# Twelve blocks of Strassen weight sums: from VectorE's program to one of GpSimd's own

## What is computed

```python
ODD_SPLITS = (RET_QK_W, RET_QK_W, RET_V_W, RET_V_W, MEM_W, MEM_W)   # 1024, 1024, 2048, 2048, 256, 256
h = rms_norm(x, norm_g)
rq, rk, rv, rz, eq, ez = _split(h @ w_in, ODD_SPLITS)
```

## Time and profile before

| | |
|---|---|
| median of three runs | 2156.94 us (2155.61 to 2162.51) |
| the profiled execution | 2156.11 us, span of its instructions 2154.3 us |
| TensorE busy | 2118.6 us, 98% of the span |
| weight loads of TensorE (beside its products) | 1171.6 us, 54% |
| VectorE busy | 755.4 us, 35% |
| ScalarE busy | 539.3 us, 25% |
| GpSimd busy | 0.2 us, four instructions |
| mean granted TensorE clock | 0.999 |

### The profile page before, as it was taken

One profiled execution on the slowest core, in us unless ns is written; L12 is line 12 of the kernel. 1 busy time (PEld: TensorE's weight loads), 2 busy tenths in 40 slices (PEclk: granted clock), 3 DMA queues, 4 the chain that ended last, 5 costly groups with the idle time before them and its releaser, 6 DMA issues.

```text
span 2154.3 us, 21143 instructions
## 1 busy us (share of the span) xinstructions
PE 2118.6 (98%) x8648; PEld 1171.6 (54%) x8648; DVE 755.4 (35%) x1215; ACT 539.3 (25%) x1065; POOL 0.2 (0%) x4
## 2 busy tenths in 40 slices
PE   8999999999999999999999999999999999999898
PEld 5555565647888777444544555554454443343247
DVE  3555544326665435312332434432140010100035
ACT  4755442320002223111223424330130100000024
POOL 0000000000000000000000000000000000000000
PEclk9999999999999999999999999999999999999999
DMA  8311211132222210233211111212639999999961
GB/s 209 76 40 40 78 40 52 45 119 79 78 80 87 74 54 22 75 80 70 96 61 61 57 40 40 72 57 78 234 137 381 409 409 409 409 409 409 409 266 40
DMA packets 162208, 316.64 MB, mean 147 GB/s; under 512 B 41216, under 2 KB 73088, under 8 KB 162112
## 3 DMA queue, kind: packets, MB, share of 16 engines
q1 hardware_dynamic: 159760, 313.29, 40.3%
q10 hardware_dynamic: 2352, 2.00, 0.4%
HBM read 312.83 MB, written 2.10 MB: 146 GB/s over the span
## 4 chain that ended last, share of the span: by engine, by line
PE 92%; DMA 4%; DVE 2%; ACT 1%; issue 1%; SPq 0%; DVEq 0%
PE bank L459 47%; PE bank L445 12%; PE bank L2701 9%; PE bank L2751 4%; PE bank L2615 2%; PE bank L2637 2%; PE bank L1262 2%; PE bank L1312 2%; PE bank L1284 2%; PE bank L1664 2%; DMA wide<-in_w_exp_up 1%; DMA ring<-in_w_exp_gate 1%; PE bank L2287 1%; PE bank L2277 1%; PE bank L2331 1%; DMA wide<-in_w_exp_down 1%
## 5 line engine op out<-in xcount | busy, mean ns | idle before, releaser
L459 PE MATMUL bank<-hT,ring 128*128 128x512 f32 (+1 forms) x1120 | 503.7, 599 | 5.8 <-DMA ring<-in_l_w_in 5.8
L459 PEld LDWEIGHTS bank<-hT,ring 128*128 128x128 f32 (+1 forms) x1120 | 205.3, 190 | 239.6 <-issue 237.1
L2701 PE MATMUL bank<-wide,xg 128*64 128x512 f32 x488 | 125.2, 595 | 4.0 <-DMA ring<-in_w_exp_gate 1.6
L445 PE MATMUL bank<-hT,ring 128*128 128x256 f32 x512 | 114.9, 379 | 0.0
L459 PE MATMUL bank<-rz,ring 128*128 128x512 f32 x256 | 111.4, 593 | 0.9 <-issue 0.9
L459 PE MATMUL bank<-ring,hT 128*128 128x512 f32 (+2 forms) x320 | 108.4, 494 | 0.0
L445 PEld LDWEIGHTS bank<-hT,ring 128*128 128x128 f32 x512 | 97.1, 190 | 17.2 <-issue 3.8
L2701 PE MATMUL bank<-ring,xg 128*64 128x512 f32 x352 | 100.5, 595 | 2.6 <-DMA ring<-in_w_exp_gate 1.5
L445 PE MATMUL bank<-l_quarter,l_quarter 128*128 128x256 f32 x384 | 87.2, 380 | 0.0
L2751 PE MATMUL bank<-wide,hidT 128*64 128x512 f32 x304 | 78.8, 596 | 3.7 <-DMA wide<-in_w_exp_down 2.9
L459 PEld LDWEIGHTS bank<-rz,ring 128*128 128x128 f32 x256 | 48.6, 190 | 62.0 <-issue 61.5
(11 more groups left out here) (474 smaller groups left out, 2766.8 us busy)
## 6 DMA issues: line engine op xcount, KB each, us to landing
wide<-in_w_exp_down SPq DMA_DIRECT2D x76, 512.0 KB, 13.5
ring<-in_l_w_in SPq DMA_DIRECT2D x18, 2048.0 KB, 7.8
wide<-in_w_exp_gate SPq DMA_DIRECT2D x68, 512.0 KB, 12.3
wide<-in_w_exp_up SPq DMA_DIRECT2D x54, 512.0 KB, 14.2
ring<-in_w_exp_up SPq DMA_DIRECT2D x50, 512.0 KB, 10.8
ring<-in_w_exp_down SPq DMA_DIRECT2D x42, 512.0 KB, 14.7
ring<-in_w_in SPq DMA_DIRECT2D x10, 2048.0 KB, 7.9
ring<-in_w_exp_gate SPq DMA_DIRECT2D x38, 512.0 KB, 13.3
```

The source lines that it names most:

```text
L445: mm = pe.matmul(self.out(n)[:, half * 256:half * 256 + 256], *halves[half][k], start=i == 0 and not job["goes_on"], stop=False, skip_grou ...
L459: mm = pe.matmul(self.out(n), *mats[i], start=i == 0, stop=i == len(mats) - 1)
L2701: mm = pe.matmul(bank[2 * which + n][e * 64:(e + 1) * 64, :], xg[p // 2 % 2][:, k, s:s + CAP], block_ap(j)[k % 2][:, n * 512:(n + 1) * 512 ...
```

## The change

The weight sums are taken out of VectorE's hooks and written as a program of GpSimd: `run_stages` gets a `gpsimd` function. It goes through the twelve blocks in order, and does for each `weight_sums` and `last_weight_sum`. GpSimd waits for the block's weights (`load_sem`), for the eviction of p4 of the block before (`free`, after which nothing reads s1 any more), and before the last sum for the eviction of p2 (`done_at[... + 2]`), which was the last reader of a12. s1 now counts on `weights_summed` too, and s2 waits for it there. The semaphore's numbers that TensorE waits for go up accordingly. Nothing else moves; the operations, their shapes and tiles are the same.

```diff
-        def run_stages(*stages):
+        def run_stages(*stages, gpsimd):
...
+                @block.gpsimd
+                def _(pool):
+                    gpsimd(pool)
...
-            def weight_sums(self, dve, j):
+            def weight_sums(self, pool, j, free):
                 a11, a12, a21, a22 = self.weights(j)
-                dve.wait_ge(*load_sem[j])
-                dveq(dve.tensor_tensor(self.s1, a21, a22, ALU.add))
-                dveq.wait(dve)
-                dve.tensor_tensor(self.s2, self.s1, a11, ALU.subtract).then_inc(weights_summed, 1)
-                dve.tensor_tensor(a21, a11, a21, ALU.subtract).then_inc(weights_summed, 1)
-
-            def last_weight_sum(self, dve, j, s2_at):
+                pool.wait_ge(*load_sem[j])
+                pool.wait_ge(*free)
+                pool.tensor_tensor(self.s1, a21, a22, ALU.add).then_inc(weights_summed, 1)
+                pool.wait_ge(weights_summed, self.before[j] + 1)
+                pool.tensor_tensor(self.s2, self.s1, a11, ALU.subtract).then_inc(weights_summed, 1)
+                pool.tensor_tensor(a21, a11, a21, ALU.subtract).then_inc(weights_summed, 1)
+
+            def last_weight_sum(self, pool, j, a12_used):
                 a12 = self.weights(j)[1]
-                dve.wait_ge(weights_summed, s2_at)
-                dve.tensor_tensor(a12, a12, self.s2, ALU.subtract).then_inc(weights_summed, 1)
-
...
+                pool.wait_ge(weights_summed, self.before[j] + 2)
+                pool.wait_ge(*a12_used)
+                pool.tensor_tensor(a12, a12, self.s2, ALU.subtract).then_inc(weights_summed, 1)
...
-                add(a21, self.b12, "dve", plus(c21, c12), [(weights_summed, w0 + 2), (quarters_made, self.first_made + 1)],
-                    hook=lambda dve, done: self.last_weight_sum(dve, j, w0 + 1))
-                add(self.s1, self.t1, "dve", plus(c22, c21),
-                    hook=None if following is None else lambda dve, done: self.weight_sums(dve, following))
+                add(a21, self.b12, "dve", plus(c21, c12), [(weights_summed, w0 + 3), (quarters_made, self.first_made + 1)])
+                add(self.s1, self.t1, "dve", plus(c22, c21))
...
-        run_stages(opening, Weave, out0, Second, lead2, Band, Linear, branches, Experts, tail, Store)
+        def weight_sums(pool):
+            free = out0.dense.done_at[cols1 - 1]
+            for dense, blocks in ((out0.dense, (1, 2, 3, 4, 5, 6, 12)), (dense1, range(7, 12))):
+                for b in blocks:
+                    j = ODD[b]
+                    q1.weight_sums(pool, j, free)
+                    q1.last_weight_sum(pool, j, dense.done_at[q1.at[j] + 2])
+                    free = dense.done_at[q1.at[j] + 4]
+
+        run_stages(opening, Weave, out0, Second, lead2, Band, Linear, branches, Experts, tail, Store, gpsimd=weight_sums)
```

More of the change, by code:

```diff
@@ L624, in __init__ @@
                 self.k, self.first_made = k, counts["quarters"] + 1
+                self.before, self.at = {}, {}
                 counts["quarters"] += 2
@@ L643, in weights, with block @@
                 return w[:, 0:k, 0:256], w[:, k:2 * k, 0:256], w[:, 0:k, 256:512], w[:, k:2 * k, 256:512]
-            def weight_sums(self, dve, j):
+            def weight_sums(self, pool, j, free):
                 a11, a12, a21, a22 = self.weights(j)
-                dve.wait_ge(*load_sem[j])
-                dveq(dve.tensor_tensor(self.s1, a21, a22, ALU.add))
-                dveq.wait(dve)
-                dve.tensor_tensor(self.s2, self.s1, a11, ALU.subtract).then_inc(weights_summed, 1)
-                dve.tensor_tensor(a21, a11, a21, ALU.subtract).then_inc(weights_summed, 1)
-            def last_weight_sum(self, dve, j, s2_at):
+                pool.wait_ge(*load_sem[j])
[5 more added lines that the diff above has]
+            def last_weight_sum(self, pool, j, a12_used):
                 a12 = self.weights(j)[1]
-                dve.wait_ge(weights_summed, s2_at)
-                dve.tensor_tensor(a12, a12, self.s2, ALU.subtract).then_inc(weights_summed, 1)
-            def block(self, jobs, j, c11, c12, c21, c22, banks=None, following=None, tokens_first=False, first=None,
+                pool.wait_ge(weights_summed, self.before[j] + 2)
+                pool.wait_ge(*a12_used)
+                pool.tensor_tensor(a12, a12, self.s2, ALU.subtract).then_inc(weights_summed, 1)
+            def block(self, jobs, j, c11, c12, c21, c22, banks=None, tokens_first=False, first=None,
                       lower=None, upper=None):
                 a11, a12, a21, a22 = self.weights(j)
-                w0 = counts["weights"]
-                counts["weights"] += 3
-                n0 = len(jobs)
+                w0 = self.before[j] = counts["weights"]
+                counts["weights"] += 4
+                n0 = self.at[j] = len(jobs)
                 def add(a, b, eng, evac, needs=(), goes_on=False, after=(), hook=None):
@@ L689, in block @@
                 add(a11, self.b11, "act", copied)
-                add(self.s2, self.t2, "dve", plus(c12, c11), [(weights_summed, w0 + 1), (quarters_made, self.first_made)], after=[0])
+                add(self.s2, self.t2, "dve", plus(c12, c11), [(weights_summed, w0 + 2), (quarters_made, self.first_made)], after=[0])
                 add(a12, self.b21, *(first or ("act", copied)), goes_on=True, after=[1])
-                add(a21, self.b12, "dve", plus(c21, c12), [(weights_summed, w0 + 2), (quarters_made, self.first_made + 1)],
-                    hook=lambda dve, done: self.last_weight_sum(dve, j, w0 + 1))
-                add(self.s1, self.t1, "dve", plus(c22, c21),
-                    hook=None if following is None else lambda dve, done: self.weight_sums(dve, following))
+                add(a21, self.b12, "dve", plus(c21, c12), [(weights_summed, w0 + 3), (quarters_made, self.first_made + 1)])
+                add(self.s1, self.t1, "dve", plus(c22, c21))
                 add(a22, self.t4, "dve", plus(c21, c21), hook=upper)
-                add(a12, self.b22, "dve", plus(c12, c12), [(weights_summed, w0 + 3)], goes_on=True, after=[2], hook=lower)
+                add(a12, self.b22, "dve", plus(c12, c12), [(weights_summed, w0 + 4)], goes_on=True, after=[2], hook=lower)
                 return n0
@@ L1504, in build @@
             first = fm1(ODD[i // 4], (i % 4) * P, to(rqk[i]), "act")
-            if i == 2:
-                jobs[first]["dve_then"] = lambda dve, done: q1.weight_sums(dve, ODD[1])
             if i == 0:
@@ L1541, in build @@
             q1.block(jobs, ODD[b], first[:, :, 0:256], first[:, :, 256:512], second[:, :, 0:256], second[:, :, 256:512],
-                     banks=banks_of[b % 3], following=ODD[b + 1], upper=turned_pair(second), lower=turned_pair(first))
+                     banks=banks_of[b % 3], upper=turned_pair(second), lower=turned_pair(first))
         def centre(c, ts, copied=None):
@@ L1564, in values_by_quarters @@
             q1.block(jobs, ODD[4 + c], v[:, 0:2, 0:256], v[:, 2:4, 0:256], v[:, 0:2, 256:512], v[:, 2:4, 256:512],
-                     banks=banks, following=following, tokens_first=True,
+                     banks=banks, tokens_first=True,
                      upper=centre(c, (0, 1), lambda: dense_of().done_at[n + 2]), lower=centre(c, (2, 3)))
         for c in range(3):
-            values_by_quarters(jobs, c, lambda: out0.dense, ODD[5 + c] if c < 2 else ODD[12], banks=banks_of[(c + 4) % 3])
+            values_by_quarters(jobs, c, lambda: out0.dense, banks=banks_of[(c + 4) % 3])
         row1 = fac1.rows[0]
@@ L1579, in build @@
         q1.block(jobs, ODD[12], eq_pair[:, :, 0:256], eq_pair[:, :, 256:512], ez_pair[:, :, 0:256], ez_pair[:, :, 256:512],
-                 banks=banks_of[1], following=ODD[7], upper=memory_scaled(ez_pair, 1.0), lower=memory_scaled(eq_pair, 0.125))
+                 banks=banks_of[1], upper=memory_scaled(ez_pair, 1.0), lower=memory_scaled(eq_pair, 0.125))
         out0 = Products(jobs, upto=ODD[12] + 2, begun=(KD, KD, KD, 2), begin=dict(act=turns["act"], dve=turns["dve"]))
         jobs = []
-        values_by_quarters(jobs, 3, lambda: dense1, ODD[8])
+        values_by_quarters(jobs, 3, lambda: dense1)
         def first_gates(c11):
@@ L1600, in build @@
             q1.block(jobs, ODD[8 + b], first[:, :, 0:256], first[:, :, 256:512], second[:, :, 0:256], second[:, :, 256:512],
-                     following=ODD[9 + b] if b < 3 else None, first=first_gates(first[:, :, 0:256]),
+                     first=first_gates(first[:, :, 0:256]),
                      upper=scaled_gates(second, 0), lower=scaled_gates(first, 256))
```

2 lines of the change are left out of this document (1 added, 1 removed).

## The result

| | before | changed |
|---|---|---|
| median of 11 runs each, made together | 2158.3 us (2155.45 to 2162.51) | 2165.25 us (2164.53 to 2167.85) |
| ratio, 95% interval | 1 | 1.0034 [1.0025, 1.0043] |
| profiled execution, span | 2156.11 us, 2154.3 us | 2167.71 us, 2165.9 us |

The account below looks back on a forecast made before the run. The prediction took TensorE, busy in 98% of the span, as the bound. Gains of -5.8 us plus +3.4 and +1.7 for collisions made -0.7 us, a forecast median of 2156.2 us, range 2150.0 to 2166.0.

Parts of the forecast that it names:

- rival 2: GpSimd gets its turn between any two VectorE instructions, without a pause: +8.0 us, 2164.9 us; chance 0.30.
- exponentials, 682 to 691 us: Block 7's last sum falls between two products, holding up reduction, exponentials and score product: +2.0 us in rival 2.
- cut near 789 us: Cut at head 1's end, about 1.1 us to spare, hit by a21 and what s2 leaves: about +2.0 in rival 2.
- cut of the third place: Scale and cut after head 2's additions: forecast removes the 1.24 us wait; rival 2 makes it 4.7 us.
- The gains, -5.8: Sums leaving VectorE shorten TensorE's waits at heads 0, 1 and 2: -3.5, -1.1 and -1.2 us.
- What bounds, and the plain stretch at no cost: TensorE bounds; from 470 to 670 us it is busy 200.00 of 200 us, so seven plain blocks gain nothing.
- The sum's length, 2.4 us, and no wait for GpSimd before p1: A GpSimd sum takes 2.4 us; under 4.7 us TensorE never waits for one, p1 being tightest.
- Additions of heads 0 and 2, +3.4 and +1.7: GpSimd sums slip in between additions of squares, each pushing the next by 1.7 us: two at head 0, one at head 2.
- The stages behind keep what is won or lost: The expert stage behind keeps the 5.8 us gain, since SyncE's transfers there move with TensorE's products.
- The step that failed: The forecast's assumption on exclusion, between none and full: GpSimd enters only in VectorE's pauses, costing +3.4 and +1.7 us.
- No cost; GpSimd waits, and has time: Second and third place: head 1's additions have no GpSimd sum beside them and scale has no pause, so 0 us.
- VectorE busy some 58 us less: Sign expected in the profile after: 48 sums of 1.22 us each leave VectorE's busy time.

Follow-up runs that it names:

- e1_tiny: Changed kernel with each GpSimd sum working on one number per partition, so the weight sums are left out: 2151.02 us, ratio 0.9969 to before.
- e2_plain: Changed kernel with only the sums of blocks 1 to 6 and 12 on GpSimd, the others back on VectorE: 2158.3 us, ratio 1.0 to before.
- e6_reorder: Kernel before, all sums on VectorE, with hooks of blocks 8 to 10 moved to a later eviction: 2152.26 us, ratio 0.9971 to before.
- e5_placed: Changed kernel with sums of blocks 7, 9, 10 and 11 waiting until VectorE's tight instructions are through: 2150.45 us, ratio 0.9969 to before.
- e7_one: Changed kernel with block 11's three sums waiting for head 3's first cut: 2159.64 us, ratio 1.0008 to before.

## Why the prediction was wrong

The forecast and rival 2 against the waits of TensorE in the trace, in us (the 0.9 and 0.2 us that every kernel has are left out):

| place | before | forecast | rival 2 | after |
|---|---|---|---|---|
| `eq` near 675 us | 0 | 0 | 0 | 0.65 |
| exponentials, 682 to 691 us | 0 | 0 | 2.0 | 1.19 |
| additions of head 0 | 3.47 | 3.4 | 3.4 | 2.73 |
| additions of head 1 | 1.07 | 0 | 0 | 0 |
| cut near 789 us | 0 | 0 | 2.0 | 1.64 |
| additions of head 2 | 0 | 1.7 | 1.7 | 1.33 |
| cut of the third place | 1.24 | 0 | 4.7 | 4.05 |
| sum | 5.78 | 5.1 | 13.8 | 11.59 |

- **The gains, -5.8: right.** With the sums out of the way and nothing in their place (e1_tiny) the stretch is 6.1 us shorter.
- **What bounds, and the plain stretch at no cost: right.** TensorE stays at 200.00, e2_plain changes nothing.
- **The sum's length, 2.4 us, and no wait for GpSimd before p1: right.** 2.35 us, and the waits have no line of GpSimd.
- **Additions of heads 0 and 2, +3.4 and +1.7: right in kind**, 2.7 and 1.3 in size. An addition is held up only by what is left of a sum when its square is ready: 1.4 us, not 1.7.
- **The stages behind keep what is won or lost: right.** From the first product over `rz` to the end of the span it is 1288.1 us before, 1288.0 after and 1288.1 in e1_tiny.
- **The step that failed:** "I take a value between: they exclude each other, and GpSimd gets in only where VectorE's list pauses." No row of before bore on who wins between queued instructions. The runs show strict turns, 8.93 us for four products with three sums between them, so that scale and cut, priced "No cost; GpSimd waits, and has time", cost 4.05 and 1.64 us, and the reduction near 682 us 1.19. That was rival 2, with a chance of 0.30 against 0.37, and its prices were a little high, 13.8 us of waits in all for 11.59.
- **Missed by both:** the wait of 0.65 us at `eq`, held up by block 7's sum of a21, and the clock. Where TensorE waited 2.7 and 4.05 us its granted clock fell afterwards. From the five short windows above: 2 x (0.46 + 0.39 + 0.28 + 0.50 + 0.08) = 3.4 us of full clock lost. So the stretch grew by 5.8 us of waits and 3.4 of clock; 0.4 of its 9.6 stays unplaced. Rival 2's 8.0 us, close to what was measured, had waits too large and no clock in it: that it came so near is in part luck. The measured 2165.25 us also lies inside the stated range, 2150.0 to 2166.0, but at the end that was put there for rival 2; the prediction gave 0.25 to anything over 2163.4.

Marks that the prediction named for exclusion, products stretched to near 3 us and evictions at 0.69, came in; the mark of rival 2 alone, a wait of 4.7 us for cut, came in with 4.05. "VectorE busy some 58 us less" was inconsistent with the prediction's own exclusion: a blocked instruction counts as busy.

## What to carry to other kernels

Moving SBUF work from VectorE to GpSimd doesn't take it out of VectorE's way: count one GpSimd instruction for each two-input VectorE instruction that is queued beside it, and compare that with the slack of whoever waits for the last of these. Place the GpSimd work behind the tight instructions by a wait, or cut it into shorter pieces. Ask first whether a later place in VectorE's own list does the same; here moving the sums' hooks in three blocks did (e6_reorder).

## What the runs showed of the hardware

- **Turns are strict, and by instruction, where both engines have work queued.** Three GpSimd sums of 2.35 us went in between four queued products (8.93 us for 2.49). Halves of 1.27 us cost the same products 3.2 us, three copies of 1.04 us with one input 2.5, and fills of 0.95 us, which read nothing, none.
- **VectorE holds up GpSimd too**, by the rest of its current instruction: 2.66 to 2.79 us for 2.35, up to 3.34.
- **The granted clock falls behind some waits.** After TensorE's wait of 2.73 us the product over `ret_sum` took 1.82 us for 1.10 and the clock stood at 0.54 and 0.61 in the next two stretches of 2 us, near the lower of its two levels, 1.2 GHz; after 4.05 us it stood at 0.72, 0.50 and 0.92 in the next three. But the wait of 3.47 us before was followed by a product of 1.10 us at full clock, so the wait's length alone doesn't decide. With the two waits the falls went too: e1_tiny, e5_placed and e6_reorder show none, and e7_one only the one behind its wait of 2.7 us. What sets them was not tried by itself.
